# First feed-forward of a trunk layer: four groups by seven quarter products, and a modulation spread over three engines

## The reference

```python
x = LN(ALPHA*x + 0.5*gate1 * ffn1(x*(1+scale1)+shift1))   # SwiGLU, 2816 hidden columns
x = LN(ALPHA*x +     gate2 * mix(x*(1+scale2)+shift2))    # gated scan and attention
x = LN(ALPHA*x + 0.5*gate3 * ffn2(x*(1+scale3)+shift3))
# shift, scale, gate = nine vectors of 1024, for two conditions v:
mod[v] = silu(c[v]) @ w_mod + b_mod                        # w_mod is 1024 x 9216, fp32
ffn(a) = (silu(a @ w_in[:, :FF]) * (a @ w_in[:, FF:])) @ w_out
```

## Time and profile before

| | us |
|---|---|
| median of 3 runs | 2564.34 (2563.31 to 2565.68) |
| span of the profiled execution | 2564.1 |
| PE busy | 2404.4 (94%) |
| DVE busy | 1909.9 (74%) |
| ACT busy | 875.2 (34%) |
| POOL busy | 454.9 (18%) |

### The profile page before, as it was taken

One profiled execution on the slowest core, in us unless ns is written; L12 is line 12 of the kernel. 1 busy time (PEld: TensorE's weight loads), 2 busy tenths in 40 slices (PEclk: granted clock), 3 DMA queues, 4 the chain that ended last, 5 costly groups with the idle time before them and its releaser, 6 DMA issues. The chain is left out here.

```text
span 2564.1 us, 38920 instructions
## 1 busy us (share of the span) xinstructions
PE 2404.4 (94%) x15844; PEld 1522.7 (59%) x15844; DVE 1909.9 (74%) x2907; ACT 875.2 (34%) x1431; POOL 454.9 (18%) x390
## 2 busy tenths in 40 slices
PE   7999999999999787999879999889999999999987
PEld 2555555555555466777757766645555666666643
DVE  3687777888666765788857778888766787878787
ACT  2511111111121244777744544623312333333221
POOL 0000000000000022222210100321862232232047
...
GB/s 337 50 99 99 89 93 99 110 91 64 83 34 81 64 63 3 25 1 1 17 48 39 48 19 63 12 132 115 83 44 60 75 75 75 73 72 67 52 56 99
DMA packets 158899, 179.97 MB, mean 70 GB/s; under 512 B 12631, under 2 KB 129267, under 8 KB 157698
## 3 DMA queue, kind: packets, MB, share of 16 engines
q1 hardware_dynamic: 158722, 177.49, 21.5%
...
## 5 line engine op out<-in xcount | busy, mean ns | idle before, releaser
L2257 PE MATMUL psum<-act_hi,ffn_win_hi 128*128 128x384 f16 x1392 | 453.8, 326 | 3.2 <-DVE ffn_win_lo L2725 2.4
L2257 PE MATMUL psum<-act_hi,ffn_win_lo 128*128 128x384 f16 x1392 | 453.8, 326 | 0.0
L2257 PE MATMUL psum<-act_lo,ffn_win_hi 128*128 128x384 f16 x1392 | 453.8, 326 | 0.0
L2524 ACT ACTIVATE ffn_silu<-psum,ffn_win_inverse 128x384 f32<-128x384 f32 x90 | 52.1, 579 | 735.1 <-PE psum L2257 732.0
L2793 DVE SCALAR_TENSOR_TENSOR Y<-psum,ffn_h_unit,Y 128x512 f32<-128x512 f32 x306 | 225.2, 749 | 86.5 <-PE psum L2303 85.9
L2303 PE MATMUL psum<-ffn_wout_hi,ffn_h_hi 128*128 128x512 f16 x720 | 279.5, 388 | 7.6 <-issue 5.4
L2303 PE MATMUL psum<-ffn_wout_lo,ffn_h_hi 128*128 128x512 f16 x720 | 278.7, 387 | 0.0
L2303 PE MATMUL psum<-ffn_wout_hi,ffn_h_lo 128*128 128x512 f16 x720 | 278.5, 387 | 0.0
L2257 PEld LDWEIGHTS psum<-act_hi,ffn_win_hi 128*128 128x128 f16 x1392 | 136.2, 98 | 93.1 <-DVE ffn_win_lo L2725 2.8
L2257 PEld LDWEIGHTS psum<-act_hi,ffn_win_lo 128*128 128x128 f16 x1392 | 136.2, 98 | 90.0
L2257 PEld LDWEIGHTS psum<-act_lo,ffn_win_hi 128*128 128x128 f16 x1392 | 136.2, 98 | 89.5
...
## 6 DMA issues: line engine op xcount, KB each, us to landing
...
w_mod<-in_w_mod SPq DMA_DIRECT2D x36, 1024.0 KB, 4.8
...
```

What stands on the lines that cost most here:

```text
L2257: last = nc.tensor.matmul(bank[:, 0:CH], win[b][w][:, half, k, :], K.A[a][:, k, c * CH:(c + 1) * CH], start=(n == 0), stop=(n == 3 * KT - 1))
L2524: nc.scalar.activation(sa[s][:], pa[s][:, 0:CH], ACT.Silu, scale=winv[:, b:b + 1]).then_inc(silu, 1)
```

## The change

1. Groups 5 to 8 of the first feed-forward go by quarter products (`Quarters(K, nc, tag, 5, 9, ...)`). POOL makes the four activation sums and the sums of eight blocks' weights. Scales leave one more bit of room. Groups 9 and 10 are as before.
2. The late modulation runs on three engines. DVE makes condition 0 only (8 steps a matrix, `steps`), ACT scales the piece in its place by condition 1 after DVE's step (`scales`, one 128x1024 activation), and POOL accumulates it (`adds`, one copy and seven additions). The ring has three slots; load n waits for POOL's addition 2(n-3)+2 (`load_late`). All matrices are summed by columns, in pieces between the matmuls of one up (`sum_piece`, 16 one-column fp32 products; `SLOTS` has the ups as (group, block, chunk)). `take` (DVE) adds the bias. Gate rows come from six transposes in up(4,1,1) and are stored in group 4.
3. PE spreads the qkv maxima ahead of up(9,1,2); the weights are loaded after group 8's products, their high halves made in group 10 ahead of gate (10,0,1), their low halves among the additions of group 10.

```diff
-    ROWS = (2, 5, 8)
...
+    ORDER = (3, 4, 6, 7, 2, 5, 8)
...
+    RING = 3
+    LOADS = len(ORDER) * KT // 2
+    SLOTS = {(1, 1, 1): 0, (1, 1, 2): 1, (2, 0, 2): 2, (2, 1, 1): 3, (3, 0, 1): 4, (3, 1, 1): 5, (4, 0, 2): 6}
...
+    def load_late(self, sp, *numbers):
+
+        for n in numbers:
+            m, k = self.ORDER[n // 4], 2 * (n % 4)
+            if n < self.RING:
+                sp.wait_ge(self.w_used, n + 5)
+            else:
+                sp.wait_ge(self.added, 2 * (n - self.RING) + 2)
+            sp.dma_start(self.ring[n % self.RING][:], self.w_mod[:, k:k + 2, m * D:(m + 1) * D]).then_inc(self.w_in[n % self.RING], 16)
...
+    def sum_piece(self, pe, n, j, bank_free):
+
+        nc, acc, bank = self.nc, self.acc[n % 2], self.p_sums[n % 2]
+        if j == 0:
+            pe.wait_ge(self.one_ok, 2)
+            pe.wait_ge(self.stepped, KT * (n + 1))
+            pe.wait_ge(self.added, KT * (n + 1))
+            bank_free()
+        for v in range(2):
+            last = nc.tensor.matmul(bank[:, 2 * j + v:2 * j + v + 1], acc[:, v, j * P:(j + 1) * P], self.one[:], start=True, stop=True)
+        if j == KT - 1:
+            last.then_inc(self.summed, 1)
...
+    def steps(self, dve, n, a, b):
+
+        nc, acc = self.nc, self.acc[n % 2][:, 0, :]
+        for k in range(a, b):
+            w, loaded, count = self.slot(n, k)
+            dve.wait_ge(loaded, count)
+            factor = self.silu[:, k, 0:1]
+            if k:
+                dve.wait_ge(self.stepped, KT * n + k)
+                ins = nc.vector.scalar_tensor_tensor(acc, w, factor, acc, ALU.mult, ALU.add)
+            else:
+                if n >= 2:
...
+    def scales(self, act, n, a, b):
+
+        for k in range(a, b):
+            w, _, _ = self.slot(n, k)
+            act.wait_ge(self.stepped, KT * n + k + 1)
+            self.nc.scalar.activation(w, w, ACT.Copy, scale=self.silu[:, k, 1:2]).then_inc(self.scaled, 1)
+
+    def adds(self, gp, n):
+
+        nc, acc = self.nc, self.acc[n % 2][:, 1, :]
+        for k in range(KT):
+            w, _, _ = self.slot(n, k)
+            gp.wait_ge(self.scaled, KT * n + k + 1)
+            if k:
+                gp.wait_ge(self.added, KT * n + k)
+                ins = nc.gpsimd.tensor_tensor(acc, acc, w, ALU.add)
+            else:
+                if n >= 2:
+                    gp.wait_ge(self.summed, n - 1)
+                ins = nc.gpsimd.tensor_copy(acc, w)
+            ins.then_inc(self.added, 1)
...
+            quarters = Quarters(K, nc, tag, 5, 9, ((end_at + Quarters.TMP, end_at + Quarters.TMP + 18432), (at, at + 18432),
+                                                   (at + 30720, at + 31872), (at + 39680, at + 40832)),
+                                end_at, at + 32768, (at + 18432, at + 24576))
...
+                if i == 2:
+                    mod.load_late(sp, 15)
...
+                if i == 1:
+                    mod.load_late(sp, 7, 8, 9, 10)
+                if i == 2:
+                    mod.load_late(sp, 16, 17, 18)
+                if i == 3:
+                    mod.load_late(sp, 24, 25, 26)
                 sp.wait_ge(in_lo, i * GB + 3)
...
+                if i == 0:
+                    mod.load_late(sp, 3, 4, 5, 6)
+                if i == 1:
+                    mod.load_late(sp, 11, 12, 13, 14)
+                if i == 2:
+                    mod.load_late(sp, 19, 20, 21, 22, 23)
+                if i == 3:
+                    mod.load_late(sp, 27)
...
+            def first_up(i, b, c):
+                n = mod.SLOTS.get((i, b, c))
+                free = lambda: pe.wait_ge(y_added, (i - 1 + b) * HPG + 3)
+                if n is not None:
+                    up(i, b, c, lambda j: mod.sum_piece(pe, n, j, free))
+                elif (i, b, c) == (4, 1, 1):
+                    up(i, b, c, lambda j: mod.turn_rows(pe, j, free))
+                else:
+                    up(i, b, c)
...
-                if 2 <= i <= 8:
-                    if mod.ORDER[i - 2] in mod.ROWS:
-                        row = mod.ROWS.index(mod.ORDER[i - 2])
...
+                if i == 2:
+                    mod.scales(act, 2, 4, KT)
+                if i == 3:
+                    mod.scales(act, 5, 0, 4)
...
+                if i == 1:
+                    mod.scales(act, 1, 0, KT)
+                if i == 2:
+                    mod.scales(act, 3, 0, KT)
+                if i == 3:
+                    mod.scales(act, 5, 4, KT)
+                    mod.scales(act, 6, 0, 5)
+                gate(i, 1, 0)
+                wout_hi(i)
+                if i == 2:
+                    mod.scales(act, 4, 0, 4)
+                if i == 3:
+                    mod.scales(act, 6, 5, KT)
+                gate(i, 1, 1)
+                if i == 1:
+                    mod.scales(act, 2, 0, 4)
+                if i == 2:
+                    mod.scales(act, 4, 4, KT)
...
                 gate(0, 1, 1)
+                mod.scales(act, 0, 0, 3)
                 gate(0, 1, 2)
+                mod.scales(act, 0, 3, KT)
...
+            def first_group(i, par):
+                last = i == NG - 1
+                steps = lambda n, a, b: mod.steps(dve, n, a, b)
+                if not last:
+                    win_max(i * GB + 2, 0, i + 1)
+                if i == 2:
+                    steps(2, 4, KT)
+                if i == 3:
+                    steps(5, 0, 4)
+                dve.wait_ge(h_lo, i * UPG - UPG)
...
+                product(i, par, 0, 1)
+                if i == 3:
+                    mod.take(dve, 4)
+                product(i, par, 0, 2)
...
+                    dve.wait_ge(y_added, (i - 1) * HPG + 3)
+                for t in range(NT):
+                    add(i - 1, t, i == 1)
+                    if i == 1 and t < KT:
+                        steps(1, t, t + 1)
+                    if i == 2 and t < KT:
+                        steps(3, t, t + 1)
+                    if i == 3 and t < 4:
+                        steps(5, 4 + t, 5 + t)
+                    if i == 3 and t >= 4:
+                        steps(6, t - 4, t - 3)
+                    if last and t < qkv.NP:
+                        qkv.weights_lo(dve, t)
+                    if last and t >= 5:
+                        dve.wait_ge(y_added, (i - 1) * HPG + 2 * t + 1)
+                        qkv.bracket(dve, t - 5)
+                if not last:
+                    win_lo(i * GB + 2, 0)
...
+                if i == 2:
+                    steps(4, 0, 4)
+                if i == 3:
+                    steps(6, 5, KT)
+                if last:
                     dve.wait_ge(y_added, i * HPG + 3)
                     qkv.bracket(dve, 4)
...
+                if i in (1, 2, 3):
+                    mod.take(dve, (0, 3, 5)[i - 1])
                 if not last:
...
+                if i == 1:
+                    steps(2, 0, 4)
+                if i == 2:
+                    steps(4, 4, KT)
...
                 product(0, 0, 1, 0)
                 wout_lo(0)
+                mod.steps(dve, 0, 0, 3)
                 product(0, 0, 1, 1)
+                mod.steps(dve, 0, 3, 6)
                 win_max(3, 1, 1)
+                mod.steps(dve, 0, 6, KT)
                 product(0, 0, 1, 2)
...
+                quarters.sums(gp, 0, False)
+                mod.adds(gp, 0)
+                mod.adds(gp, 1)
+                quarters.sums(gp, 1, False)
+                for n in range(2, len(mod.ORDER)):
+                    mod.adds(gp, n)
+                weight_sums(quarters.first_block)
+                gp.wait_ge(mod.summed, 6)
+                quarters.sums(gp, 2, True)
+                quarters.sums(gp, 3, True)
+                for blk in range(quarters.first_block + 1, quarters.first_block + quarters.blocks):
+                    weight_sums(blk)
+                gp.wait_ge(quarters.products, quarters.PER * quarters.blocks)
                 qkv.pool(gp)
                 att.pool(gp)
```

466 lines of the change are left out of this document (217 added, 249 removed).

## The result

| | before | changed |
|---|---|---|
| median | 2564.97 (4 runs, 2563.31 to 2565.68) | 2596.52 (4 runs, 2594.67 to 2599.76) |
| ratio | 1 | 1.0128, 95% interval 1.0113 to 1.0142 |
| span of the profiled execution | 2564.1 | 2597.8 |

The change makes the kernel slower by 31.6 us. 2597.5 had been forecast.

The account below looks back on a forecast made before the run. PE was taken to bound the kernel, so any wait of PE lengthens it. From 2564.1 us, savings of 30.4 and added waits of 13.0, 8.8, 19.2, 17.0 and 5.8 gave 2597.5; range 2540 to 2622.

Parts of the forecast that it names:

- sums on PE: Late modulation: today's 35.8 us goes, seven column sums at 4.04 and six transposes come in; -6.2 us.
- quarter groups: Groups 5 to 8 by quarter products: 65.71 us each against 70.77, change of form taken as 0; -20.2 us.
- group 2: Additions slowed by sharing, +4.4 us, and PE's wait for matrix 2's sum in up(2,0,2), +19.2.
- opening: Opening group: load 3 behind POOL's first activation sum delays DVE's steps and the hidden maximum; +13.0 us.
- groups 3 and 4: Group 3's 16 steps each 0.8 us longer, scalings and additions of matrices 4 and 6 late; +17.0 us.
- clock: The clock falls behind each of two long waits, 2.9 us each; +5.8 us.
- Matrix 2: up(2,0,2): PE waits for steps, ACT's scaling and POOL's additions of this sum; +19.2 us, without sharing +10.9.
- upper end: DVE's step waits for a whole POOL addition each time: a pair takes 4.9 us, total 2642.
- Taking turns: DVE steps and POOL additions share their way to SBUF: together 3.4 us; additions out of PSUM are untouched.
- Rival 1: Engines hardly disturb each other; only the order of work makes PE wait: 2548.9 us, faster; chance 0.24.
- Rival 3: Sharing holds, but half of its waits fall into DVE's idle time: 2566 us; chance 0.15.
- Rival 4: One-column products take the clock to 1.2 GHz in the ups holding them: 54.6 on top, 2652 us; chance 0.05.

Follow-up runs that it names:

- experiment 11: Experiment 10 with POOL adding only 64 of the 1024 columns, order and waits kept: 2536.62 us, ratio 0.9885.
- Experiment 1: Changed kernel with only matrix 2's sum and its take moved from up(2,0,2) to up(2,1,0): 2587.96 us, ratio 1.0101.
- experiment 10: Experiment 5 with the first activation sum in the opening again, matrix 0's steps 6 and 7 later, finished-column work at group 9's start: 2564.28 us, ratio 0.9997.
- experiment 4: Changed kernel with POOL adding only 64 of the 1024 columns, all waits and the order kept: 2561.72 us, ratio 0.9995.
- experiment 5: Changed kernel with matrix 2's sum later, matrix 0's additions before the first activation sum, and DVE steps moved into idle time: 2573.22 us, ratio 1.0036.

## Why the prediction was right

The main waits are those of the forecast, in the places where it had put them. That the time is only 1.0 us from it is luck: the sums on PE were off by 9.3 us one way, the quarter groups by 2.9, group 10 by 2.8 and group 2 by 7.2 the other (by 4.3 with the one fall of the clock that was forecast for it apart). The terms, against the marks:

| term | forecast | measured | from |
|---|---|---|---|
| four quarter groups | -20.2 | -17.3 | 265.74 - 4 x 70.77; 65.71 in three, 68.60 in the last |
| sums on PE | -6.2 | -15.5 | 35.8 less 7 x 2.9; group 1 of experiment 11 takes 76.54, 5.8 over 70.77 for two |
| group 9 | -4.0 | -3.0 | 72.67 - 75.70 |
| group 10 | 0 | +2.8 | 68.75 - 65.97 |
| opening | +13.0 | +11.4 | 133.09 - 121.68 |
| group 1 | +4.4 | +4.8 | 81.41 - 70.77 - 5.8 |
| group 2 | +23.6 | +30.8 | 107.33 - 70.77 - 5.8 |
| groups 3 and 4 | +17.0 | +18.1 | 168.32 - 141.54 - 3 x 2.9 |
| clock | +5.8 | in the lines above | |
| sum | +33.4 | +32.1 | 32.0 at the last spread, 33.7 in the span |

- **What bounds the kernel** held: PE had no slack, and its waits are the loss.
- **The opening** went step by step: the sum forecast to end at 116.6 ended at 116.7, the load forecast for 126.2 let DVE go at 126.04. Steps 6 and 7 took 4.6 and not 6.8, since POOL held only one of the two up.
- **Matrix 2** waited 20.8 us for 19.2 forecast, and of the parts the steps, ACT and the additions are there in this order. (The forecast's last sum, 16.7 + 1.14 + 4 x 2.35, gives 27.2 and not 27.5.) Experiment 1 shows what the term did not say: when this wait goes, some 11 us of other waits come up behind it, so the sum's place was worth 8.6 us and not 20.8.
- **Additions**: the cycle was forecast as 3.4 and is 3.30 in the changed kernel. The forecast's upper end, a step that waits for nearly a whole addition each time (4.9), is real too: 4.68, five times in a row in experiment 10. Which of the two would come the forecast had no reason to know.
- **Taking turns.** Experiments 4 and 11 take POOL's long additions away and leave their order: 34.8 and 27.7 us; in experiment 11 nothing but the turns is left to explain it. Steps (2.05 for 1.28) and low halves (9.11 for 3.26) wait, additions out of PSUM (1.40) do not. The Trainium skill, in GPSIMD Engine Reference, § 1 Specifications, names such a contention with GpSimd for DVE instructions with two SBUF inputs, or in a 2-port performance mode. The trace agrees.
- **Mis-sized**: the sums on PE. I took 4.04 us each, the price of one that stands alone; among other matmuls it is 2.9, and the clock stays up. This error of 9 us was balanced by others: the last quarter group, 2.9 longer than the three ahead of it and taken as 0 (PE is busy 67.47 us in it and 65.43 in the group before it; its waits are 0.28 and 0.85); group 10, +2.8, where DVE's qkv low halves and gated additions now share one group; and more falls of the clock than the two counted, among them one at the mark of group 3, behind a wait of 4.79 (322 to 330 us, clock 0.50).
- **The rivals.** Rival 1 (order alone) is refuted as the whole story, but experiment 4 shows that about half of the waits need no long addition of POOL. Rival 3 (half of the waits falls into DVE's idle time) is not what the changed kernel does, but what experiments 5 and 10 make of it by moving steps there: 2573.22 and 2564.28, against its 2566. Rival 4 (clock) did not happen: two sums cost 5.8 us, and 290 to 296, with a sum in it, has a clock of 1.00.

What stays open: experiment 10's own executions differ by 12 us among themselves, where the kernel before has 9. The two cycles of a tile, 3.30 and 4.68, with the same order of work could do this, and they are seen in different kernels; that they change from one execution of a kernel to the next is not shown, since each kernel has one profile.
